# Experts' gate and up as seven block products, the modulation moved into the out-projection, one weight difference on GpSimd

## What is computed

```
mod = silu(c) @ w_ada[l] + b_ada[l]            # 6 rows of 1024; the second block has its own w_mod
x   = x + gate1 * (concat(heads, conv) @ w_out[l])
n   = rms_norm(x);  h = n * gain + shift       # gain, shift from mod
for e in range(16):                            # each expert takes its best 128 rows
    rows   = top 128 of softmax(h @ w_router)[:, e]
    hidden = silu(h[rows] @ w_gate[l, e]) * (h[rows] @ w_up[l, e])
    x[rows] += weight[rows] * gate2 * (hidden @ w_down[l, e])
```

## Time and profile before

| | |
|---|---|
| runs shown | 3: 4182.42, 4183.13, 4183.99 us |
| median | 4183.13 us |
| the profiled execution, span from first to last instruction | 4181.3 us |
| PE busy | 3922.6 us, 94% |
| DVE, ACT, POOL busy | 1727.1, 825.6, 394.2 us |
| DMA | 682.22 MB, mean 163 GB/s |

### The profile page before, as it was taken

The page is one execution under the profiler, slowest core; times in us unless marked ns, Lnnn a source line. Parts: engine busy times, 40 slices in busy tenths (PEclk is TensorE's granted clock), DMA queues, the critical chain, the costliest instruction groups (busy, mean ns, idle before and its releaser), DMA issues. The chain is left out here.

```text
span 4181.3 us, 37629 instructions
## 1 busy us (share of the span) xinstructions
PE 3922.6 (94%) x14996; PEld 1907.0 (46%) x14996; DVE 1727.1 (41%) x2387; ACT 825.6 (20%) x1606; POOL 394.2 (9%) x407
## 2 busy tenths in 40 slices
PE   7989987999999899996999999899988999999998
PEld 4444443444444444442444444344467444444443
DVE  5778532111111488635011111145544244333576
ACT  2144321010110225421100101033343110000000
POOL 2000000000000000000000000000021022222541
PEclk9999998999999999997999999999999999999999
DMA  8210129999997301024999999521000211111464
GB/s 295 76 41 1 46 93 335 359 348 347 353 339 238 116 1 41 1 76 168 330 347 354 343 350 347 158 85 35 21 28 23 81 51 41 40 51 41 166 200 162
DMA packets 236091, 682.22 MB, mean 163 GB/s; under 512 B 16656, under 2 KB 80784, under 8 KB 235920
## 3 DMA queue, kind: packets, MB, share of 16 engines
q1 hardware_dynamic: 226416, 646.27, 42.8%
q0 software_dynamic: 9504, 33.56, 3.4%
HBM read 637.83 MB, written 41.94 MB: 163 GB/s over the span
## 5 line engine op out<-in xcount | busy, mean ns | idle before, releaser
L1618 PE MATMUL ps<-w_ring,h_act 128*128 128x512 f32 x3008 | 1302.0, 593 | 13.4 <-ACT h_act L1713 12.1
L1618 PEld LDWEIGHTS ps<-w_ring,h_act 128*128 128x128 f32 x3008 | 568.1, 190 | 720.2 <-issue 700.5
L1759 DVE SCALAR_TENSOR_TENSOR h_act<-ps,gate,gate_row 128x1024 f32<-128x1024 f32 x30 | 38.5, 1283 | 746.3 <-PE ps L1618 746.3
L3213 PE MATMUL ps<-h_act,arena_two 128*128 128x512 f32 x704 | 313.2, 592 | 1.8 <-ACT h_act L410 0.9
L937 DVE SCALAR_TENSOR_TENSOR y<-y,par_one 128x1024 f32<-128x1024 f32 x240 | 307.5, 1281 | 3.9
L1701 ACT ACTIVATE h_act<-ps 128x1024 f32<-128x1024 f32 x32 | 32.8, 1026 | 1172.9 <-PE ps L1618 1172.9
L3213 PE MATMUL ps<-arena_two 128*128 128x512 f32 x528 | 237.4, 592 | 0.0
L2055 PE MATMUL ps<-h_act,arena_two 128*128 128x512 f32 x544 | 235.1, 592 | 1.0 <-DVE h_act L421 1.0
L604 PE MATMUL ps<-h_act,arena_a 128*128 128x512 f32 x512 | 221.5, 593 | 4.2 <-DVE h_act L421 2.0
L1752 DVE TENSOR_TENSOR h_act<-h_act,ps 128x1024 f32<-128x1024 f32 x32 | 39.1, 1221 | 446.2 <-PE ps L1618 446.2
L1568 POOL DMA_INDIRECT h_act<-n_rows,idx x32 | 31.3, 977 | 1924.0 <-DVE idx_halves L1745 1238.1
(11 more groups left out here) (458 smaller groups left out, 4677.2 us busy)
## 6 DMA issues: line engine op xcount, KB each, us to landing
w_ring<-in_w_gate SPq DMA_DIRECT2D x128, 1024.0 KB, 8.5
w_ring<-in_w_up SPq DMA_DIRECT2D x128, 1024.0 KB, 7.0
w_ring<-in_w_down SPq DMA_DIRECT2D x128, 1024.0 KB, 5.2
arena_two<-in_ffn_w_down SPq DMA_DIRECT2D x44, 1024.0 KB, 4.9
w_mod<-in_w_ada SPq DMA_DIRECT2D x48, 512.0 KB, 6.2
w_mod<-in_w_mod SPq DMA_DIRECT2D x48, 512.0 KB, 6.5
arena_two<-in_ffn_w_up SPq DMA_DIRECT2D x22, 1024.0 KB, 5.1
arena_b<-in_w_ada SPq DMA_DIRECT2D x32, 512.0 KB, 4.5
```

What stands on the lines that cost most here:

```text
L1618: last = nc.tensor.matmul(ps[:, bank + i, :], lhs[:, k * P:(k + 1) * P], ring[:, c, k % kp, i * HALF:(i + 1) * HALF], start=(k == 0), stop ...
L3213: last = nc.tensor.matmul(ps[:, q % 8, :], left[:, k, :], right[k], start=k == 0, stop=k == KH - 1)
```

## The change

**Gate and up.** The 128 rows and the 1024 inner and outer columns of gate and up are halved, and each product of 2x2 blocks is made by seven block products instead of eight (m1, m2, m6, m5, m7, m3, m4 in PE's order). A block product takes 64 stationary columns (64 rows of tokens) and 512 moving ones, 4 steps of k, for gate (output partitions 0 to 63) and up (64 to 127) in turn: 8 matmuls. The sums of token blocks (four, 128x256) are DVE's. The weight blocks need four differences each for gate and up, 128x2048: first, second and fourth on DVE, the third on POOL; for expert 0 the first three are all on POOL, ahead of the first gather. The block results are combined by accumulating in PSUM, with three copies by ACT (`snap_m1`, `snap_u2`, `snap_m5`) and three additions by DVE, and silu and multiplication are made in four parts of 64x512.

**Loads.** Gate and up come as quarters (1 MB each, eight an expert), laid out beforehand so that 8 KB lie together per partition; down in four pieces as before, also 8 KB together. A quarter is loaded again when the block product or difference that reads it last is done.

**Modulation.** The 48 pieces are loaded and added in the out-projection, by POOL's queue, into three slots; DVE's additions are put between its other work by `fill(n)`, and PE's totals at four places. `gate1` is doubled, since the next block's is made while this one's is read.

```
+    totals = {(5, 1): (2,), (6, 1): (3,), (7, 6): (4, 5)}
...
+            @block.gpsimd
+            def _(pool):
+                mod.load_bias(pool)
+                for n in range(mod.n_pieces):
+                    mod.load(pool, n)
...
+                    if t:
+                        pe.wait_ge(weighed, t)
+                        mod.total(pe, t - 1, 2 * (t - 1))
...
+                fill(14)
                 dve.wait_ge(x_loaded, 16)
                 dve.wait_ge(ch_back, 2 * KC)
                 for t in range(3):
                     add(t)
+                    if t:
+                        mod.keep(dve, t - 1, 2 * (t - 1))
+                    if t < 2:
+                        fill(2 + t)
...
+                def block_product(out, left, right, begins):
+                    for k in range(KH1):
+                        for w in range(2):
+                            last = nc.tensor.matmul(out[w * TOK:(w + 1) * TOK, :], left[:, k, :], right[:, w, k, :],
+                                                    start=begins and k == 0, stop=k == KH1 - 1,
+                                                    skip_group_check=not begins)
+                    return last
...
+                def m1(e):
+                    landed_quarter(pe, e, B11)
+                    pe.wait_ge(xeT_kept, KD * (e + 1))
...
+                def m6(e):
+                    pe.wait_ge(m1_kept, e + 1)
+                    pe.wait_ge(s_made, 4 * (e + 1))
+                    pe.wait_ge(t2_made, 2 * (e + 1))
+                    block_product(in_z(e), sums[:, S2], t2, False).then_inc(m6_done, 1)
...
+                def third_difference(e, w):
+                    pool.wait_ge(landed[4 * w + B22], 16 * (e + 1))
+                    pool.wait_ge(t1_made, 2 * e + w + 1)
+                    nc.gpsimd.tensor_tensor(raw[:, w, B12], raw[:, w, B22], raw[:, w, B12], ALU.subtract).then_inc(t3_made, 1)
...
                         pool.wait_ge(xe_turned, e + 3)
                         gather(e + 4)
                     if e < final:
+                        for w in range(2):
+                            third_difference(e + 1, w)
                         pool.wait_ge(ye_kept, e + 1)
...
+                    for w in range(2):
+                        first_difference(dve, nc.vector.tensor_tensor, e + 1, w)
+                    corner_11(e + 1)
+                    token_sums(e + 1)
+                    for w in range(2):
+                        second_difference(dve, nc.vector.tensor_tensor, e + 1, w)
+                    dve.wait_ge(down_used, PER * (e + 1))
```

More of the change, by code:

```diff
@@ L181, in __init__ @@
         self.n_pieces = KD * len(rows)
-        self.biases = sum(v in self.GATES for v in rows)
+        self.b_cols = b_cols
+        self.biases = sum(v in self.GATES for v in rows) + (b_cols is not None)
     @staticmethod
@@ L1419, in weigh, with fill @@
                                             ALU.mult).then_inc(aff_ready, 1)
+                pieces = [0]
+                def fill(n):
+                    for _ in range(min(n, mod.n_pieces - pieces[0])):
+                        mod.add(dve, pieces[0])
+                        pieces[0] += 1
                 nc.vector.scalar_tensor_tensor(core.gain[:], core.mod[:, scale_at:scale_at + KD], 1.0, gains,
@@ L1485, in experts, with load_down @@
+def load_down(eng, down, landed, mats, e, c):
+    eng.dma_start(down[:, c], mats[2][e, c]).then_inc(landed[8 + c], 16)
+def experts(core, raw, t1, t2, down, landed, mats, affT, stored, idx, gate, n_rows, x_rows, shift_at, next_one):
     nc = core.nc
-    per, kp = PER, KPP
-    GATE, UP, DOWN = 0, 1, 2
     final = N_EXP - 1
     rows = 2 * N_EXP
-    def pieces(e):
-        return min(mod.n_pieces, -(-mod.n_pieces * (e + 1) // (N_EXP - 2))) if e >= 0 else 0
-    def totals(e):
-        return range(pieces(e - 2) // KD, pieces(e - 1) // KD)
@@ L1553, in _ @@
-                mod.load_bias(sp)
-                reload(GATE, 1)
-                reload(UP, 1)
-                for e in range(1, N_EXP):
-                    for n in range(pieces(e - 2), pieces(e - 1)):
-                        mod.load(sp, n)
+                for i in (B11, B12, B22, B21):
+                    for w in range(2):
+                        load_quarter(sp, raw, landed, mats, 0, w, i)
+                for c in range(PER):
+                    load_down(sp, down, landed, mats, 0, c)
@@ L1559, in _ @@
                     if e < final:
[L1560 to L1563 removed]
+                        again_first(e + 1)
+                    for c in range(PER):
+                        sp.wait_ge(down_used, PER * (e - 1) + c + 1)
+                        load_down(sp, down, landed, mats, e, c)
             @block.gpsimd
@@ L1764, in _ @@
-                    for n in range(pieces(e - 1), pieces(e)):
-                        mod.add(dve, n)
                 dve.wait_ge(scattered, 16 * final)
@@ L1771, in _ @@
                                                    ALU.mult, ALU.mult).then_inc(ye_kept, 1)
-                for i in totals(final):
-                    mod.keep(dve, i, 6)
-                for n in range(pieces(final - 1), pieces(final)):
-                    mod.add(dve, n)
+                if next_one is not None:
+                    dve.wait_ge(one_loaded, 16)
 T_U, T_V, T_XR, T_YG = 0, KA, 2 * KA, 2 * KA + KB
```

378 lines of the change are left out of this document (257 added, 121 removed).

## The result

The changed kernel takes 4226.28 us (median of 4 runs, 4222.89 to 4231.23), the kernel before beside it 4182.77 (4 runs, 4180.11 to 4183.99): a ratio of 1.0099 with a 95% interval of 1.0085 to 1.0114. It is slower by 1%. The forecast was 4157, and the range ended at 4218.

What follows compares the result with a forecast made beforehand. PE was taken to bound the kernel (busy 595.5 of 600 us in the experts). Experts -69.8, start +8.8 and out-projection +35.2 sum to -25.8: 4155.5 us on the span, 4157 on the median, range 4098 to 4218.

Steps and rivals of the forecast that it cites:

- Block products: Gate and up in the experts: 56 matmuls of 64 columns, column halves fully overlapped, 24.2 us in place of 27.6 an expert.
- (c): The 56 matmuls: column halves don't fully overlap, so slower; 4268 us at 1.75 overlap, 4930 at none; chance 0.16.
- POOL's differences: Third differences in the experts: 4.5 us for each 128x2048, DVE and POOL each waiting for the other's running instruction.
- (a): Experts: POOL doesn't hold DVE up for its whole instruction, 24 cycles 2.1 us shorter, 4107 us; chance 0.15.
- (d): Experts: weights come late because the quarters' releases stop the queue; every 1 us a cycle is 31 us; chance 0.05.
- (b): Larger sizes: a POOL-queue piece takes 7 us (4193 us), or POOL's difference 5.2 (4191 us); chance 0.17.
- The cycle of twelve experts: First twelve experts of a layer: DVE's chain, pushed back by POOL, sets 42.5 us, where PE alone needs 40.4.
- DVE gets one sum in: Experts, between POOL's two third differences of 4.5 us: DVE makes one token sum, and POOL's second difference ends at 37.6.
- The start: Each layer before the first expert: later first gather (+1.5, second layer +2.7), m1's wait for token columns (+2.3); +8.8 together.
- That the search isn't blocked: Layer start: DVE's search reads one operand in SBUF, so no blocking by POOL was counted; otherwise +12 more a layer.
- The out-projection: Out-projection with the modulation: 11 us of totals on PE and 6.6 of waits, 17.6 a layer, +35.2.

Runs made afterwards that it cites:

- third_late: The change, but POOL starts its third differences only when DVE has finished both second differences of that expert; 4112.56 us, ratio 0.9833.
- thirds_chained: The change with one wait added: POOL's second third difference waits until the first is counted; 4211.31 us, ratio 1.0077.
- mod_only: The kernel before with only the modulation moved into the out-projection as in the change, experts otherwise as before; 4208.78 us, ratio 1.0066.
- one_on_pool: third_on_dve, but one of the two third differences an expert (up's) stays on POOL; 4109.48 us, one run.
- pool_reads: third_on_dve plus four chained POOL additions of 128x896 an expert on an unused array, at the third differences' old place; 4110.07 us, one run.
- pool_writes: third_on_dve plus ten POOL fillings of 128x896 with zeros an expert, at the third differences' old place; 4104.91 us, one run.
- third_on_dve: The change, but DVE makes the third differences behind the second ones, POOL only those of expert 0; 4108.64 us, ratio 0.9828.
- halves_apart: The change, but each block product does four matmuls of gate, then four of up, instead of one each in turn; 4296.7 us, ratio 1.0272.
- fill_twelve: third_on_dve with 12, 4 and 3 modulation additions around add(0) and add(1) in the out-projection, in place of 14, 2 and 3; 4108.56 us, ratio 0.9821.

## Why the forecast was wrong

- **Block products: right.** 3.46 us each was forecast for full overlap and is what is measured. Rival (c) fell. The cycle that PE sets is 40.0 us (forecast 40.4).
- **POOL's differences: right in size.** 4.5 us each, and they hold DVE, as read from the earlier trace rows. Rivals (a) and (d) fell; (b) too, since a difference took 4.5 and a piece 4.8 us in the median (4.4 was said, 7 in the rival), and the 14th addition ended 1 us sooner than forecast.
- **The cycle of twelve experts: the step that failed.** The forecast is 40.4 of PE and 2.1 of waiting, 42.5. Measured are 40.0 of PE, 3.0 of waiting and 1.3 to 3.0 by which the products behind the wait are longer, 44.6 on the mean. From the first m6 to the 13th it is 1234.25 - 699.31 = 534.9 us where 510 was forecast: 11.0 more in the 12 waits (36.2 for 25.2), 18.8 in the products behind them, 4.9 less in PE's own cycles.
  - The larger part is **the clock behind the wait**, which no term of the sum had. It was put at nothing, without a reason.
  - The smaller part is the order of DVE and POOL. The forecast has DVE done with the first corner and two of the four token sums when POOL takes hold at 28.2, "DVE gets one sum in, POOL holds 4.5 again", then one sum and the second differences. third_late shows the stretch undisturbed: the corner's multiplication ends 845.29 + 0.69 - 818.49 = 27.5 after m6, as forecast (27.4), but POOL's gather is so early (844.91) that its differences would start at 27.4. So the multiplication is caught, and all four sums are left behind POOL: 27.4 + 9.0 + 0.55 + 1.5 + 4.5 = 42.9, 0.4 more than forecast, and PE is ready 0.4 sooner. In the change all of this lies 1.4 us later after m6 by the clock: POOL starts at 815.75 - 786.93 = 28.8, the second differences end at 44.3. That DVE gets one instruction in between was wrong for this code, but thirds_chained shows that this alone hardly matters: the hold is as long.
- **The rest of the first layer's experts.** 24.9 of the 29.2 missing lie in the twelve cycles, 1.7 before them (m1(0) took 5.35 us), 1.0 in the last three, 1.6 at the end (the last down 15.70 us in place of 14.0). The second layer is missing 30.5.
- **The start: +5.9 and +7.0, forecast +3.8 and +5.0.** That m1 waits for eight token columns is 2.3 as forecast. That the search isn't blocked held for its scans (0.66 us beside POOL as before), but not for its last instruction, the addition, which was put at nothing: 3.7 us. The forecast had 1.5 there in the first layer, for POOL's differences themselves.
- **The out-projection: +20.0 and +14.8, forecast +17.6 each.** The sum, 34.8 for 35.2, is right with some luck: mod_only, with the same code, has +20.1 and +19.1.
- **The range** ended at 4218, and 4226 was measured. From above it was bounded by the sizes alone (a piece of 7 us, a difference of 5.2). What was missing is a bound by the hold itself: what if DVE is caught one instruction sooner, and what if the clock falls after the wait.

The experts are 59.7 of the 66.5 us by which the span was missed, the start 4.1, the untouched stages 3.1.

Shown by runs: that POOL's additions and subtractions stretch DVE's instructions and its fillings don't (one_on_pool, pool_reads, pool_writes); that PE's wait follows by a margin of 6.5 us, read in third_on_dve, in the change, one_on_pool, pool_reads and thirds_chained; and that without the collision the change is 1.7% faster than the kernel before, by either way of avoiding it. Only read from traces: that the clock falls because of the wait; no run changed one without the other, and in the out-projection it fell without a wait. Open: DVE's held instruction is recorded 0.6 us ahead of POOL's and loses all the same (815.13 and 815.75).

## What to carry to other kernels

When work is handed to GpSimd because VectorE is the fuller engine, look at what VectorE has to do in exactly that time, and take the whole length of GpSimd's two-operand instructions as lost to it: the same two instructions cost 114 us in front of VectorE's due work, and behind it the experts were as fast as without them. Work out the margin (here 6.5 us from VectorE's last needed result to TensorE's reading it) and compare the hold with it, since under the margin a hold is free and above it everything goes to the bound, with a surcharge for TensorE's clock. In a forecast, put a price on TensorE's clock behind every short wait that you foresee: here it cost more (18.8 us a layer) than the error in the waits themselves (11.0).

## What the runs showed of the hardware

- Beside a POOL instruction with two operands in SBUF, a DVE instruction of 0.69 us took 5.70 (one of 4.5), 10.14 (two back to back), 2.13 (several of 1.9, each waiting for the last). The Trainium skill says that a DVE instruction with two SBUF inputs contends with a GpSimd instruction that reads SBUF, not with one that only writes it (SBUF — State Buffer, "Who interferes with whom"); the trace agrees (5.70 beside a subtraction, 0.69 beside fillings). That POOL's back-to-back instructions let nobody in, and that a wait between them does, is from these runs.
- Not held: DVE beside POOL's fillings (0.69 beside 8.99 us of them), DVE's scans of 32x512 (0.66 beside POOL's subtractions), and `ye` of 128x1024 with one operand in PSUM (1.28 beside them). Held: the addition of 32x128 to a column (3.98 in place of 0.28); why, no run shows.
- TensorE's two column halves overlap in full with 512 moving columns: eight matmuls of 64 stationary columns take 3.46 us. In halves_apart matmuls of two successive products started 0.05 us apart, so a half of the next product ran beside one of this.
- After idle times of 3 us TensorE's clock was mostly low for a while (8.4 to 10.1 us for two products in place of 7.1), but not always (7.09 at one of thirds_chained's waits), and not after pool_reads' four waits of up to 0.9 us. It was also low, 0.57 on the mean of 4 us, behind matmuls with one moving column where TensorE hadn't waited (third_on_dve, 620 to 624), and 1.00 at the same place in fill_twelve.
